# Forty-two products of the identity with itself on TensorE, at the entry of an RWKV layer and ahead of the last query turn of a band attention

## The reference

```
x = x + 0.5 * rms_norm(f, ffn2_post_g)        # f: the second feed-forward layer's output
h = rms_norm_2(x, ln_mix[0])
xx = token_shift(h) - h
xs = h[None] + xx[None] * mu[:, None, None, :]
r, k, v = einsum('nbtc,ncd->nbtd', xs[:3], w_rkv)
```

```
q = rms_norm_2(h @ wq, q_gain) * 64 ** -0.5
s = q @ k.T - alibi ;  p = softmax(s, sink) ;  o = p @ v ;  out = o @ wo
```

## Time and profile before

| | us |
|---|---|
| median of 3 executions | 1398.0 |
| lowest, highest | 1397.31, 1400.11 |
| the profiled execution: its time | 1399.79 |
| the profiled execution: its span, first to last instruction | 1397.6 |
| TensorE busy in the span | 1362.7 |
| mean granted TensorE clock (1 is full speed) | 0.996 |

### The profile page before, as it was taken

One profiled execution on the slowest core, in us unless ns is written; L12 is line 12 of the kernel. 1 busy time (PEld: TensorE's weight loads), 2 busy tenths in 40 slices (PEclk: granted clock), 3 DMA queues, 4 the chain that ended last, 5 costly groups with the idle time before them and its releaser, 6 DMA issues.

```text
span 1397.6 us, 23649 instructions
## 1 busy us (share of the span) xinstructions
PE 1362.7 (98%) x8859; PEld 1115.1 (80%) x8859; DVE 855.7 (61%) x1235; ACT 697.1 (50%) x1110; POOL 38.1 (3%) x42
## 2 busy tenths in 40 slices
PE   8999999999999999999899999999999998999998
PEld 6888877778888878888687688778888887788887
DVE  4544567975755464445784788656555677565554
ACT  5444456575465464444553444235444556644442
POOL 0000000000000000000001000110000010000000
PEclk9999999999999999999999999999999999999999
DMA  8655546556454565555352100315555651265552
GB/s 295 215 185 180 180 131 210 166 180 203 161 165 154 150 206 193 196 194 181 114 196 76 61 4 33 112 35 167 184 186 182 227 178 51 89 211 190 184 183 104
DMA packets 145535, 220.53 MB, mean 158 GB/s; under 512 B 16760, under 2 KB 65166, under 8 KB 145328
## 3 DMA queue, kind: packets, MB, share of 16 engines
q1 hardware_dynamic: 145456, 219.43, 47.7%
HBM read 218.33 MB, written 1.05 MB: 157 GB/s over the span
## 4 chain that ended last, share of the span: by engine, by line
PE 87%; DVE 6%; ACT 3%; issue 1%; DMA 1%; POOL 1%; SPq 0%; POOLq 0%; ACTq 0%; DVEq 0%
PE acc L291 12%; PE acc L293 12%; PE acc L292 12%; PE gp L291 12%; PE gp L293 12%; PE gp L292 11%; PE gp L2761 2%; PE tp L942 1%; PE acc L2776 1%; DVE sb_w_lo L280 1%; DMA sb_raw<-in_ffn_w 1%; ACT sb_w_hi L264 1%; PE acc L1279 1%; PE tp L291 1%; ACT sb_arena L407 1%
## 5 line engine op out<-in xcount | busy, mean ns | idle before, releaser
L280 DVE TENSOR_TENSOR sb_w_lo<-sb_raw,sb_w_hi 128x1024 fp32r<-128x1024 f32 (+1 forms) x380 | 451.8, 1215 | 207.3 <-ACT sb_w_hi L264 205.7
L264 ACT ACTIVATE sb_w_hi<-sb_raw 128x1024 fp32r<-128x1024 f32 (+1 forms) x380 | 388.1, 1053 | 212.6 <-PE acc L293 106.8
L291 PE MATMUL gp<-sb_w_hi,sb_xa_hi 128*128 128x512 f32 (+1 forms) x752 | 299.3, 398 | 8.4 <-DVE sb_xa_lo L2338 4.5
L293 PE MATMUL gp<-sb_w_lo,sb_xa_hi 128*128 128x512 f32 (+1 forms) x752 | 292.4, 389 | 0.0
L292 PE MATMUL gp<-sb_w_hi,sb_xa_lo 128*128 128x512 f32 (+1 forms) x752 | 291.9, 388 | 0.0
L291 PEld LDWEIGHTS gp<-sb_w_hi,sb_xa_hi 128*128 128x128 f32 x752 | 141.7, 188 | 42.5 <-DVE sb_w_lo L280 7.2
L293 PEld LDWEIGHTS gp<-sb_w_lo,sb_xa_hi 128*128 128x128 f32 x752 | 141.5, 188 | 29.7
L292 PEld LDWEIGHTS gp<-sb_w_hi,sb_xa_lo 128*128 128x128 f32 x752 | 141.8, 189 | 27.3 <-issue 0.5
L291 PE MATMUL acc<-sb_w_hi,sb_mid_hi 128*128 128x512 f32 x400 | 156.2, 390 | 0.0
L293 PE MATMUL acc<-sb_w_lo,sb_mid_hi 128*128 128x512 f32 x400 | 155.8, 389 | 0.0
L292 PE MATMUL acc<-sb_w_hi,sb_mid_lo 128*128 128x512 f32 x400 | 155.6, 389 | 0.0
(11 more groups left out here) (414 smaller groups left out, 1751.0 us busy)
## 6 DMA issues: line engine op xcount, KB each, us to landing
sb_raw<-in_ffn_w SPq DMA_DIRECT2D x264, 256.0 KB, 4.3
sb_raw<-in_mlp_w SPq DMA_DIRECT2D x256, 256.0 KB, 2.9
sb_raw<-in_w_in SPq DMA_DIRECT2D x72, 256.0 KB, 3.3
sb_raw<-in_a_w_rkv SPq DMA_DIRECT2D x48, 256.0 KB, 4.0
sb_raw<-in_xattn_w_kv SPq DMA_DIRECT2D x32, 256.0 KB, 3.6
sb_raw<-in_w_out SPq DMA_DIRECT2D x16, 256.0 KB, 3.3
sb_raw<-in_xattn_w_q SPq DMA_DIRECT2D x16, 256.0 KB, 3.0
sb_raw<-in_xattn_w_o SPq DMA_DIRECT2D x16, 256.0 KB, 3.1
```

The source lines that it names most:

```text
L264: A.e.activation(w_hi[:, s, :, 0:n], raw[:, r, :, 0:n], ACT.Copy).then_inc(hi_done, 1)
L280: V.e.tensor_tensor(w_lo[:, s, :, 0:n], raw[:, r, :, 0:n], w_hi[:, s, :, 0:n].bitcast(F32), ALU.subtract).then_inc(lo_done, 1)
L291: e.matmul(dst, xh, wh, start=start, stop=False)
L293: return e.matmul(dst, xh, wl, start=False, stop=stop)
```

## The change

A function `pe_idle` is added that issues n products of the constant identity with itself, fp32, 128x128 by 128x128, into the first 128 columns of a bank that it is given. Nothing reads them; each bank is written anew afterwards with `start=True`. Thirty go at the very start of `pe_mixed`, into gp 0, ahead of `pe_r_token(T, 0, 0)`. Twelve go into `pe_turn_q` for the last unit, into tp 1, behind its first wait (`biased`) and ahead of its second (`q_rows`). No wait, DMA or other instruction is added, removed or moved.

```
             def pe_mixed(self, T):
+                self.pe_idle(T, gp[:, 0, 0:P], 30)
                 self.pe_r_token(T, 0, 0)
                 self.pe_h_turn(T, 1, 0)
                 self.pe_h_turn(T, 1, 1)
...
+            def pe_idle(self, T, bank, n):
+                for _ in range(n):
+                    T.e.matmul(bank, ident, ident, start=True, stop=True)
...
             def pe_turn_q(self, T, u, free):
 
                 T.e.wait_ge(*stage(*free))
+                if u == 3:
+                    tmix.pe_idle(T, self.turn_bank(u)[:, 0:P], 12)
                 T.e.wait_ge(self.q_rows, u + 1)
```

## The result

The changed kernel has a median of 1400.19 us over 20 executions, the kernel before 1398.21 us over 20: +1.98 us, a ratio of 1.0013 with an interval of 1.0007 to 1.0019. The forecast was no change, 1398.0 us. The time lies within the range that was given, but the interval leaves out "no change": the kernel is slower by more than the measurement is uncertain. The profiled execution took 1401.92 us, with a span of 1399.8; before it was 1399.79 and 1397.6.

A forecast was written before the change was run, and what follows sets the result against it. The prediction took TensorE, busy 98% of the span, as the bound, with time only in its gaps or low clock. Entry +0.09 and attention -0.10 summed to 0.0 us, so 1398.0 us; range 1396.3 to 1400.7 us.

The forecast's parts named there:

- The price of a product: In both places, an identity product takes two records of 0.114 us, 0.228 us at full clock.
- The overshoot that uses up the cover at the entry: At the entry, the thirty end 3.04 us past the r products' old start, against 2.95 us of idle and clock time.
- +0.09: At the entry, the turn of t = 1 starts at 688.50 instead of 688.41 us, passed on undiminished.
- ScalarE as the end of the attention's chain: In the attention, ScalarE's copies, no longer TensorE, set the gain of 0.10 us.
- The granted clock of 1.00 through both places: The profile after should show full clock throughout 683 to 687 and 1167 to 1171 us.
- the fourth rival: Attention: the clock falls later, in the products from 1171.7 us on; +1.7 us, 1399.7 us, chance 0.07.
- a stall of the instruction stream: Upper bound given at the entry: TensorE waits for instructions by 1.0 us, 1399.0 us, chance 0.05.
- The third rival: Attention: timed executions' slow stretch begins later, on dense products; 0 to -1.7 us saved, middle 1397.2 us, chance 0.13.
- The first, the clock not held: Entry and attention: identity products don't keep the clock up; together +5.9 us, 1403.9 us, chance 0.07.
- The second, time coming back in full: The low clock's time is regained, 1.77 us at the entry and 1.9 in the attention; -3.7 us, 1394.3 us, chance 0.06.

The follow-up runs named there:

- before_again: The kernel before, run again unchanged for a second profile and the noise; 1397.88 us, ratio 0.9999.
- pad60: The kernel before with 60 waits on a long-reached semaphore added to TensorE's stream ahead of the core; 1400.78 us, ratio 1.0008 to before.
- pad120: The kernel before with 120 waits on a long-reached semaphore added to TensorE's stream ahead of the core; 1399.84 us, ratio 1.0003 to before.
- pad190: The kernel before with 190 waits on a long-reached semaphore added to TensorE's stream ahead of the core; 1400.52 us, ratio 1.0016 to before.
- entry30_only: The changed kernel without the twelve products in the attention, only the thirty at the entry kept; 1400.82 us, ratio 1.0016 to before.
- attn12_again: The changed kernel without the thirty products at the entry, only the twelve kept, second run; 1399.86 us, ratio 1.0008 to before.
- spread_after: The changed kernel with SyncE's burst of six weight chunks let through one at a time; 1397.11 us, ratio 0.9988 to before.
- spread_before: The kernel before with SyncE's burst of six weight chunks let through one at a time; 1397.08 us, ratio 0.9989 to before.
- after_again: The changed kernel, run again unchanged for a second profile; 1400.90 us, ratio 1.0010 to before.
- pad120_again: The kernel before with 120 waits on a long-reached semaphore in TensorE's stream ahead of the core, second run; 1400.52 us, ratio 1.0014 to before.
- after_pad136: The changed kernel with 136 waits on a long-reached semaphore added, moving the core's code by 256 instructions in all; 1399.19 us, ratio 1.0000 to before.
- attn12_only: The changed kernel without the thirty products at the entry, only the twelve kept, first run; 1399.39 us, ratio 1.0004 to before.

## Why the prediction was wrong

**What held.** The price of a product, nearly (forecast 0.114 us a record: from the first of the 60 to the r products there are 6.61 us, where 6.85 was forecast, so 0.110; the 6.86 of the row has the tail of the last in it. The 24 took 2.78 to the next group, 2.74 was forecast). The overshoot that uses up the cover at the entry, all but 0.16 us of it: the turn waited for ScalarE's scaled identity still (688.50 forecast, 688.82 with everything 0.42 late, so 688.40, and no +0.09). ScalarE as the end of the attention's chain, now with 1.39 us of waiting. The granted clock of 1.00 through both places, as in these windows of PE, after:

```profile
1170.00:1171.00 1.00, 1.00 (x12) 1.00 0.00 0
1171.00:1172.00 1.00, 1.00 (x12) 1.00 0.00 0
1173.00:1174.00 1.00, 0.05 (x1) 1.00 0.94 313
```

From 1170.65 to 1172.6 TensorE did nothing but transposes there and then idled for 1.39 us, and the clock stayed up: the fourth rival did not come about. It says little about transposes and the clock, though, because in before_again the clock stayed up too, with idle times of 1.73, 0.41 and 1.34 us and nothing but transposes between them. The Trainium skill's page TensorE: Matmul & The Clock Gate, section Part 4: PE-mode transpose, says that transposes don't count for the clock. What bears on that is the row that the prediction used, the clock's return at 1171.1 with nothing but transposes since 1167.45, and it does so in three more profiles at the same place (pad60, pad120, pad190).

**The step that failed** is the one on a stall of the instruction stream: "above, a stall of the instruction stream. The longest such wait of TensorE is 1.0 us, and I take it as the upper end", with 0.05 of chance, and "No DMA or wait is added or moved on SyncE's or GpSimd's queue", which looks at two queues and not at TensorE's own instructions. I treated the wait of the earlier trace rows as a sample of what could happen among the new products. It was a wait at the edge of an instruction block, for a transfer held up by a burst of weights, and what the new instructions do is move the code under the edge. The stall became 1.69 us in place of 0.96, outside the upper end of 1.0 that was set for it, and the two parts of the core took 1.84 us more, far from both sets of products. Two questions were not asked: what the transfers of instructions run into at 889 us, which SyncE's issues and the DMA share show, and by what part of a block 120 instructions move the edges. The sign of the answer could hardly have been had beforehand, I think. That something like the 1.0 us of the wait was at stake could.

**How 2.0 us come out of it.** With the clock full in the second part, both parts together take 24.96 us (entry30_only) and 24.82 (pad120) with the moved stream, against 23.57 (before_again) and 23.56 (attn12_again): 1.25 to 1.4 us. That is the wait: the change's adds 1.9 us to the first part (17.33 less the 15.44 of spread_after), the one in before_again 0.76 to the second (8.25 less the 7.49 of spread_before). With the low clock in it, 27.21 and 27.01 (the change, after_again) stand against 25.37: 1.6 to 1.8. The second part of the change's profile shows the clock:

```profile
896.00:897.00 1.00, 0.90 (x40) 0.98 0.97 356
897.00:898.00 1.00, 1.00 (x17) 0.50 0.19 53
903.00:904.00 1.00, 1.00 (x17) 0.61 0.00 0
```

It is at half, 1.2 GHz, for 6.8 us, from 897.0 to 903.8, where before it was for 3.4, from 898.0. At half for 3.4 us costs 1.8 us in the second part (10.05 against 8.25), for 6.8 us 2.4 (9.88 against the 7.50 of pad120), so the longer fall adds 0.6 to the 1.25 of the wait. Whether the clock falls there at all differs from execution to execution of one kernel: it fell in pad120_again and not in pad120. How long goes with the stream, in all ten profiles in which it fell behind 895: 3.4 us in the five with the wait ahead of record 2490 or 2493, 6.8 us in the five with it ahead of 2434 or 2463. Why is not shown.

**The twelve.** The profiles show what they do. The stretch from the values of unit 0 to the wait for ScalarE takes 7.22 us where the clock falls there (before), 6.76 where it doesn't (entry30_only, 1163.65 to 1170.41), and 7.16 with the twelve, whatever the clock would have done (the change; attn12_again, 1163.27 to 1170.43). So they gain 0.06 in one kind of execution and cost 0.40 in the other. That was missed: the prediction costed them against the profiled execution alone, in which the clock had fallen. The third rival considered executions in which it falls later, never those in which it doesn't fall. Of the ten profiles without the twelve, five don't fall there and four do as before. In the tenth, spread_before, the clock is at half from 1166.8 to 1173.6, well into the products behind, and that profile loses 1.8 us on before between 1150 and 1180: the third rival, once in ten. Weighed by these ten, the twelve cost and gain about nothing. The two sets of the twelve alone came out 1.4 and 1.65 us high at the median. One by one their intervals reach down to no difference, but the means of both together are 1.0 us up, give or take 0.5, and chance alone is a poor account of that. Against it, spread_after and after_pad136 have the twelve and no such cost, and the change is not slower than the thirty alone. No run explains it, and it stays open.

**The rivals.** The first, the clock not held, did not happen in any of the seven profiles with the thirty whole products. (Its sum left five of the twelve's records at the low rate; from 1165.7 it is six or seven, some 0.3 us more, which changes nothing in the choice.) The second, time coming back in full, did not either: both waits on ScalarE stayed, 0.16 and 1.39 us. The first and the fourth had the right sign and nothing else. The stall of the instruction stream, at 1399.0 and with 0.05 of chance, was the right kind of event, looked for in the wrong place and set too short.

## What to carry to other kernels

Instructions that cost nothing where they stand still move all the code behind them. Where an engine consumes straight-line code quickly, look for waits without a releaser, and for what the DMA engines do a few microseconds ahead of them, before costing an edit of a hundred instructions at zero. A pad of idle instructions with the same count is the control that tells the edit's work from its place. The cure is on the other side: a queue that lets go of a burst of loads as soon as one unrelated wait is met should be made to issue what has a free buffer earlier, one piece at a time.

## What the runs showed of the hardware

- TensorE's instructions come during the execution by transfers of 16.4 KB on a queue that shares the sixteen DMA engines with the weights. That is 256 instructions of the 64 bytes that the Trainium skill's page Trainium Architecture — The Big Picture, section The software stack, gives an instruction, and the block edges in the core bear it out: with 60 and 120 instructions more the wait stands 30 and 59 records earlier, with 190 more, at the next edge, 33 later, and with 256 more where it was. That section describes the streams as moved into the engines when the program is loaded; the trace shows 55 transfers spread over the execution. With 3 MB of weights issued from 885.8 to 892.4 a transfer came at 893, and at 890 without them; with the moved stream at 892, and at 889 without them.
- Full DMA engines make the difference: the core's other edges, one in 5 us and nearly all with DMA shares near 0 (0.00 to 0.03), pass without a wait in the profile before.
- A product of one column takes as long as one of 128 in fp32 with a weight load each (0.11 us a record at full clock), and it did not keep the clock up: that fell at 682.0 and was back at 692.1.
- The same idle time of 3.63 us at the entry lowered the clock at 683.0 in one execution and at 687.95 in another (attn12_only), where an idle time of 2.76 us had come between. There it lay on the turn of t = 1 and cost 1.7 us. That is one of the nine profiles without the thirty. In the seven with thirty whole products in place of the idle time the clock is full there, so in executions of that kind they may gain; no run was made to tell how many there are.
